# Gate and up biases copied into PSUM by ScalarE ahead of the first product, instead of one-hot products on TensorE

## The reference

```python
def clamped_swiglu(gu):
    gate, up = gu[..., :D_FF], gu[..., D_FF:]
    gate = jnp.minimum(gate, SWIGLU_LIMIT)
    up = jnp.clip(up, -SWIGLU_LIMIT, SWIGLU_LIMIT)
    return (up + 1.0) * (gate * jax.nn.sigmoid(SWIGLU_ALPHA * gate))
...
    def run_block(args):
        xb, e = args
        gu = xb @ w_gate_up[e] + b_gate_up[e]
        return clamped_swiglu(gu) @ w_down[e] + b_down[e]
```

## Time and profile before

| | us |
|---|---|
| timed runs (3) | 1540.11, 1543.22, 1545.4; median 1543.22 |
| the profiled execution: span from its first to its last instruction | 1541.1 |
| PE busy | 1519.2 (99%) |
| DVE busy | 1323.1 (86%) |
| ACT busy | 1092.0 (71%) |
| POOL busy | 238.7 (15%) |

### The profile page before, as it was taken

How to read it: one execution, slowest core, us unless ns; L and a number is a source line. 1 busy time by engine, 2 the same in 40 slices (tenths; PEclk the granted TensorE clock), 3 DMA queues, 4 the chain that set the end, 5 groups by cost and what they waited for, 6 DMA issues and landing times.

```text
span 1541.1 us, 21502 instructions
## 1 busy us (share of the span) xinstructions
PE 1519.2 (99%) x7332; PEld 1240.0 (80%) x7332; DVE 1323.1 (86%) x1056; ACT 1092.0 (71%) x1194; POOL 238.7 (15%) x170
## 2 busy tenths in 40 slices
PE   8999999998999999999999999999999999999997
PEld 6888789886888888888888888888888888888884
DVE  5586587747999999999999999999999999999985
ACT  6355587225777777777777777777777878777763
POOL 2611345300000011000000000011000001000111
PEclk9999999998999999999999999999999999999999
DMA  8330002446999999999999999999999999999973
GB/s 302 123 110 28 1 1 82 181 153 238 381 375 379 375 372 385 371 369 381 381 376 380 374 378 377 376 382 372 367 374 378 380 379 377 384 375 376 381 248 122
DMA packets 131102, 467.93 MB, mean 304 GB/s; under 512 B 12024, under 2 KB 12544, under 8 KB 130976
## 3 DMA queue, kind: packets, MB, share of 16 engines
q1 hardware_dynamic: 118720, 435.45, 74.1%
q0 software_dynamic: 9936, 27.01, 7.3%
q10 hardware_dynamic: 2416, 5.07, 0.9%
HBM read 452.81 MB, written 24.12 MB: 309 GB/s over the span
## 4 chain that ended last, share of the span: by engine, by line
PE 95%; DVE 2%; ACT 2%; issue 0%; DMA 0%; DVEq 0%; ACTq 0%
PE ps L1540 28%; PE ps L1542 28%; PE ps L1541 28%; PE ps L1853 2%; PE ps L1834 2%; PE ps L1826 2%; PE ps L1598 1%; PE ps L1641 1%; PE ps L1642 1%; PE ps L1771 0%; PE ps L1583 0%; DVE chunk_lo L1374 0%; ACT probs L815 0%; PE ps L1615 0%; PE ps L1616 0%; PE ps L1619 0%
## 5 line engine op out<-in xcount | busy, mean ns | idle before, releaser
L1374 DVE TENSOR_TENSOR chunk_lo<-chunk,chunk_hi 128x2048 fp32r<-128x2048 f32 x384 | 858.8, 2283 | 37.5 <-ACT chunk_hi L931 35.9
L931 ACT ACTIVATE chunk_hi<-chunk 128x2048 fp32r<-128x2048 f32 x378 | 723.1, 1914 | 103.6 <-PE ps L1542 103.6
L1540 PE MATMUL ps<-chunk_hi,XT 128*128 128x512 f32 x1024 | 404.1, 395 | 1.9 <-DVE XT L1416 1.9
L1542 PE MATMUL ps<-chunk_hi,XT 128*128 128x512 f32 x1024 | 399.5, 390 | 0.0
L1541 PE MATMUL ps<-chunk_lo,XT 128*128 128x512 f32 x1024 | 399.4, 390 | 0.0
L677 POOL DMA_INDIRECT sum_rows<-y,idx x31 | 81.4, 2626 | 952.8 <-ACT y L1059 863.7
L1540 PEld LDWEIGHTS ps<-chunk_hi,XT 128*128 128x128 f32 x1024 | 192.4, 188 | 40.9 <-DVE XT L1416 2.4
L1542 PEld LDWEIGHTS ps<-chunk_hi,XT 128*128 128x128 f32 x1024 | 192.2, 188 | 40.3
L1541 PEld LDWEIGHTS ps<-chunk_lo,XT 128*128 128x128 f32 x1024 | 192.5, 188 | 38.7
L1540 PE MATMUL ps<-chunk_hi,hidT 128*128 128x512 f32 x512 | 199.3, 389 | 0.5 <-DVE hidT L1423 0.5
L1541 PE MATMUL ps<-chunk_lo,hidT 128*128 128x512 f32 x512 | 199.2, 389 | 0.0
(11 more groups left out here) (288 smaller groups left out, 1949.8 us busy)
## 6 DMA issues: line engine op xcount, KB each, us to landing
chunk<-in_w_gate_up SPq DMA_DIRECT2D x256, 1024.0 KB, 8.4
chunk<-in_w_down SPq DMA_DIRECT2D x128, 1024.0 KB, 6.8
raw<-in_w_in SPq DMA_DIRECT2D x14, 1024.0 KB, 5.1
xs<-in_x SPq DMA_DIRECT2D x8, 512.0 KB, 6.4
w_out<-in_w_out SPq DMA_DIRECT2D x4, 1024.0 KB, 6.1
raw<-in_w_branch_a SPq DMA_DIRECT2D x2, 1024.0 KB, 5.4
raw<-in_w_branch_b SPq DMA_DIRECT2D x2, 1024.0 KB, 6.2
sum_rows<-xs ACTq DMA_DIRECT2D x4, 512.0 KB, 2.6
```

The costliest lines, as they stand in the source:

```text
L931: a.activation(chunk_hi[hi_slot(c, nxt)][:, :], chunk[c][:, :], ACT.Copy).then_inc(ex_hi, 1)
L1374: v.tensor_tensor(chunk_lo[c][:, :], chunk[c][:, :], chunk_hi[hi_slot(c, nxt, first)][:, :].bitcast(F32), ALU.subtract).then_inc(ex_lo, 1)
L1540: mm(dst, lhsT(0), rhs(0), start=start, stop=False)
L1542: return mm(dst, lhsT(1), rhs(0), start=False, stop=stop)
```

## The change

The bias products, `pick`, the bias table, its preparation on POOL, its store and its load go. In their place:

- SP loads the expert's gate bias and up bias, one row of 1024 float32 each, into one partition of `bias_rows` (the first expert's into `bias_first`): the gate row ahead of the loads of chunks 0 to 3, the up row ahead of those of chunks 4 to 7.
- POOL spreads each row over 128 partitions of `bias_all` (`partition_broadcast`), after the gather of the item has landed and ahead of the scatter: first the up row of the next expert, then the gate row of the one after that.
- ACT copies the spread rows into PSUM: `seed_gate` into banks 0 and 1 behind `rows_out`, `seed_up` into banks 2 and 3, with 1 added, behind the split of `hidT`.
- PE waits for these copies instead of adding the bias, and its first product of a bank adds to what lies there. For the banks to be in the adding state the first time, three filler products are made in them (`bits_set`).
- The scatter counter starts one DMA lower (`ADDED`), and a few start semaphores are joined.

```diff
@@ -181,7 +179,7 @@
...
-        ADDED = 3 * 16
+        ADDED = 2 * 16
...
@@ -345,6 +343,16 @@
...
+        def load_gate_row(sp, n, e):
+            sp.wait_ge(spread_g, n)
+            sp.dma_start(bias_rows[32:33, :], b_gate_up[0, bass.ds(e, 1), 0:FF]).then_inc(row_g_in, 16)
+        def load_up_row(sp, n, e):
+            sp.wait_ge(spread_u, n)
+            sp.dma_start(bias_rows[64:65, :], b_gate_up[0, bass.ds(e, 1), FF:2 * FF]).then_inc(row_u_in, 16)
         def load_expert(sp, c, e):
             sp.dma_start(chunk[c][:, :].rearrange("p (k n) -> p k n", k=2), expert_src(e, c)).then_inc(expert_in[c], 16)
@@ -449,6 +457,8 @@
...
             sp.wait_ge(merged, KD)
+            sp.dma_start(bias_first[32:33, :], b_gate_up[0, 0:1, 0:FF]).then_inc(row_g_in, 16)
+            sp.dma_start(bias_first[64:65, :], b_gate_up[0, 0:1, FF:2 * FF]).then_inc(row_u_in, 16)
             load_expert(sp, 1, 0)
...
@@ -457,11 +467,11 @@
...
             sp.wait_ge(gathered, 16)
             for c in range(8, 12):
                 load_expert(sp, c, 0)
+            load_gate_row(sp, 1, 1)
+            load_up_row(sp, 1, 1)
             for c in range(4):
                 sp.wait_ge(ex_used, c + 3)
                 load_expert(sp, c, 1)
...
@@ -472,12 +482,14 @@
...
                 load_expert(sp, c, 1)
             with sp.Fori(1, last_item) as i:
+                load_gate_row(sp, i + 1, (i + 1) % E)
                 for c in range(4):
                     sp.wait_ge(ex_used, 12 * i + c - 1)
                     load_expert(sp, c, (i + 1) % E)
                 for c in range(8, 12):
                     sp.wait_ge(ex_used, 12 * i + c - 5)
                     load_expert(sp, c, i % E)
+                load_up_row(sp, i + 1, (i + 1) % E)
                 for c in range(4, 8):
                     sp.wait_ge(ex_used, 12 * i + c + 3)
...
@@ -533,42 +544,9 @@
...
             pool.dma_start(acc[SEQ:ROWS, :], zeros[:, :]).then_inc(scattered, 16)
-
-
-            for q in range(3):
-                rows = slice(32 * q, 32 * q + 32)
-                pool.dma_start(bias32[rows, :], b_gate_up[0]).then_inc(bias_in, 16)
...
-            link(g.tensor_scalar(bias32[0:96, FF:2 * FF], bias32[0:96, FF:2 * FF], 1.0, None, ALU.add))
-            link(g.tensor_copy(bias_new[0:96, :], bias32[0:96, :]))
-            for rows in (part1, part2):
-                link(g.tensor_tensor(bias32[rows, :], bias32[rows, :], bias_new[rows, :], ALU.subtract))
-                link(g.tensor_copy(bias_new[rows, :], bias32[rows, :]))
-            link(g.tensor_tensor(bias32[part2, :], bias32[part2, :], bias_new[part2, :], ALU.subtract))
-            pool.dma_start(bias_parts, bias_new[:, :]).then_inc(scattered, 16)
@@ -645,6 +623,13 @@
...
+            pool.wait_ge(wout_ps, 2 * NT)
+            pool.wait_ge(row_g_in, 16)
+            g.partition_broadcast(bias_all[:, 0, :], bias_first[32:33, :]).then_inc(spread_g, 1)
+            pool.wait_ge(row_u_in, 16)
+            g.partition_broadcast(bias_all[:, 1, :], bias_first[64:65, :]).then_inc(spread_u, 1)
+            pool.wait_ge(spread_g, 1)
+            pool.wait_ge(spread_u, 1)
             pool.wait_ge(rows_stored, 2 * NT * 16)
             pool.wait_ge(scattered, ADDED)
...
@@ -652,12 +637,29 @@
...
+            def spread_gate(n):
+                pool.wait_ge(row_g_in, 16 * n + 16)
+                pool.wait_ge(gate_seeded, n)
+                pool.sem_inc(pool_past, 1)
+                g.partition_broadcast(bias_all[:, 0, :], bias_rows[32:33, :]).then_inc(spread_g, 1)
+            def spread_up(n):
+                pool.wait_ge(row_u_in, 16 * n + 16)
+                pool.wait_ge(up_seeded, n)
+                pool.sem_inc(pool_past, 1)
+                g.partition_broadcast(bias_all[:, 1, :], bias_rows[64:65, :]).then_inc(spread_u, 1)
             pool.wait_ge(idx_ready, 1)
             gather(0)
             pool.wait_ge(idx_ready, 2)
             pool.wait_ge(xt_ps, 1)
             pool.sem_inc(pool_past, 1)
             gather(1)
+            pool.wait_ge(gathered, 32)
+            spread_gate(1)
+            pool.wait_ge(spread_g, 2)
             pool.wait_ge(items_ready, 1)
             items = pool.value_load(items_i[0:1, 0:1], min_val=E, max_val=E * PASSES)
             lead = pool.value_load(items_i[0:1, 2:3], min_val=E - 4, max_val=E * PASSES - 4)
@@ -668,6 +670,15 @@
                 pool.wait_ge(xt_ps, n + 2)
                 pool.sem_inc(pool_past, 1)
                 gather((u + 2) % 4)
+            def spread_next(n, gate=True):
+                pool.wait_ge(gathered, 16 * n + 48)
+                spread_up(n + 1)
+                if gate:
+                    spread_gate(n + 2)
+                    pool.wait_ge(spread_g, n + 3)
+                pool.wait_ge(spread_u, n + 2)
             def scatter(n, u):
@@ -680,9 +691,11 @@
             with pool.Fori(0, lead, 4) as i4:
                 for u in range(4):
                     gather_ahead(i4 + u, u)
+                    spread_next(i4 + u)
                     scatter(i4 + u, u)
             for u in range(3):
                 gather_ahead(lead + u, u)
+                spread_next(lead + u, u < 2)
...
@@ -1007,6 +1020,26 @@
...
+            def seed_gate(n):
+                act.wait_ge(spread_g, n + 1)
+                if isinstance(n, int) and n == 0:
+                    act.wait_ge(bits_set, 1)
+                else:
+                    act.wait_ge(glu_ready, n)
+                a.activation(ps[0:CAP, 0:2, :].rearrange("p t n -> p (t n)"), bias_all[:, 0, :],
+                             ACT.Copy).then_inc(gate_seeded, 1)
+            def seed_up(n):
+                act.wait_ge(spread_u, n + 1)
+                if isinstance(n, int) and n == 0:
+                    act.wait_ge(bits_set, 2)
+                else:
+                    act.wait_ge(clip_ready, n)
+                a.activation(ps[0:CAP, 2:4, :].rearrange("p t n -> p (t n)"), bias_all[:, 1, :], ACT.Identity,
+                             bias=one[:, 0:1]).then_inc(up_seeded, 1)
             act.wait_ge(first_rows, 1)
             a.activation(f5[:, 0:2], idx_ps[:, 0:2], ACT.Copy).then_inc(first_f, 1)
             act.wait_ge(first_f, 1)
@@ -1029,6 +1062,7 @@
             act.wait_ge(idx_ready, 2)
             act.wait_ge(logits_ps, NT)
             index(2, slice(2, 3))
+            seed_gate(0)
             rows_hi(1, 0)
             rows_hi(1, 1)
             act.wait_ge(gateT_ps, 1)
@@ -1036,6 +1070,7 @@
             act.wait_ge(rows_stored, 2 * NT * 16)
             first_split_hi(4)
             first_split_hi(5)
+            seed_up(0)
             for c in (6, 7):
                 ex_split_hi(0, c)
             def sigmoid(used):
@@ -1067,6 +1102,7 @@
                 if before:
                     rows_out(i - 1, 12 * i + 6)
                 if nxt:
+                    seed_gate(i + 1)
                     ex_split_hi(i + 1, 2)
                     rows_hi(i + 2, 0)
                     ex_split_hi(i + 1, 3)
@@ -1083,6 +1119,8 @@
                     index_parts(i + 3, bass.ds((i + 3) % 4, 1))
                 ex_split_hi(i, 10, nxt)
                 hidden_hi(i + 1)
+                if nxt:
+                    seed_up(i + 1)
                 ex_split_hi(i, 11, nxt)
                 if nxt:
                     act.wait_ge(scattered, 16 * i + ADDED)
@@ -1796,9 +1832,12 @@
...
             pe.wait_ge(iota_set, 1)
+            for bank in range(2):
+                last = mm(ps[:, bank, :], onesb[:, :], iota_all[:, 0:256].bitcast(BF16), start=True, stop=True)
+            last.then_inc(bits_set, 1)
             for c in range(NT):
                 if c == NT - 1:
-                    unread(2, 1)
+                    unread(2, 2)
...
@@ -1843,30 +1882,23 @@
                     for t in range(2):
                         last = mm_split(ps[0:CAP, bank + t, :], lambda p: src[:, p, 2 * q + k, :],
                                         lambda p: expert_w(c, h, p, k, t),
-                                        start=(start and k == 0), stop=(stop and k == 1))
+                                        start=(start and k == 0), stop=(stop and k == 1), seeded=(bank < 4))
                 return last
-            def add_bias(e, bank, part, start=False):
-                for t in range(2):
-                    col = part * FF + t * 512
-                    mm(ps[0:CAP, bank + t, :], pick[:, bass.ds(e, 1)].to_broadcast([128, CAP]),
-                       bias_tab[:, col:col + 512], start=start, stop=False)
-            unread(3, 1)
+            unread(3, 2)
...
@@ -1874,18 +1906,19 @@
...
-                    add_bias(0, 0, 0)
-                weigh(c, c, c, XT, 0, c == 0, c == 3).then_inc(ex_used, 1)
-            pe.wait_ge(gateT_out, 1)
+                if c == 0:
+                    pe.wait_ge(gate_seeded, 1)
+                if c == 2:
+                    pe.wait_ge(gateT_out, 1)
```

(12 more changed lines are left out.)

89 lines of the change are left out of this document (30 added, 59 removed).

## The result

| | before | after |
|---|---|---|
| timed runs, median us | 1542.93 (1540.11 to 1545.4, 4 runs) | 1576.24 (1574.14 to 1581.11, 4 runs) |
| profiled execution, span us | 1541.1 | 1576.3 |
| PE busy | 1519.2 (99%) | 1517.7 (96%) |
| POOL busy | 238.7 (15%) | 473.6 (30%) |

The change makes the kernel slower: ratio 1.0224, 95% interval 1.021 to 1.0239. I had forecast 1515.2 with a range of 1510 to 1545. The time is 61 us above the one and 31 above the end of the other. All ratios are made of fast runs; two slow ones of the kernel before (2475.32 and 8758.93 us, beside e10 to e13) are left out.

The account below looks back on a forecast made before the run. PE was taken to set the pace at 35.47 us an expert. Span 1541.1 - 28.8 for bias products + 0.8 for fillers = 1513.1; from the timed 1543.2, less 28.0, 1515.2 us, range 1510 to 1545.

Parts of the forecast that it names:

- the one on the up seed: ACT's copy of the up bias could delay chunk 11's split by 1.05 us plus its row wait; cost on path 0.
- Bias products: On PE, 64 pairs of bias products at 0.45 us go, all on the chain: 28.8 us saved.
- the fillers' 0.8: Three filler products on PE at the start, 0.25 us each, rounded up to +0.8 us if all on the path.
- Seeds 1.05 us each: 64 ACT copies from SBUF to PSUM, 2.1 us an expert within 7.69 idle; cost on path 0.
- Spread 1.2 us: One GpSimd spread of a bias row over partitions takes 1.2 us, with 2.6 kept as the upper figure.
- DVE held for 1.2 us an expert: One spread holds up one DVE split; DVE then needs 34.4 of 34.57 us an expert, cost 0.
- Loads: SP's weight loads plus two 4 KB rows would keep up at 386 GB/s, with some 9 us in hand.
- Transfers that bind: Rival: 376 GB/s is all there is, so the beat falls back to 35.47 us; 1534 us, chance 0.10.
- both spreads on DVE: Rival: both spreads of an expert hold up DVE splits, DVE needs 35.6 us; 1544 us, chance 0.13.
- the long spread: Rival: a spread takes 2.6 us, holding DVE; 1551 us with one hit, about 1625 with two; chance 0.10.
- the third: Third rival listed: a spread of 2.6 us holds up DVE's splits, 1551 to about 1625 us; chance 0.10.
- PE waiting for a seed: Sign named as showing the forecast wrong: PE waits for ACT's copy of a bias into PSUM; no size given.

Follow-up runs that it names:

- e10: Changed kernel, with DVE waiting for its own previous split before the second and third of its three splits in a row: 1520.65 us, ratio 0.9853.
- e13: Changed kernel with both the up seed moved behind the split of chunk 5 and DVE waiting for its own splits: 1520.86 us, ratio 0.9852.
- e5: Changed kernel with the up seed later in ACT's queue, behind the split of the next expert's chunk 5: 1515.8 us, ratio 0.9818.
- e12: Kernel before the change, with two unused 128x512 reductions on DVE at the start of each item, so its splits begin later: 1541.25 us, ratio 0.9991.
- e11: Changed kernel with a 128x1 copy on DVE between the splits of chunks 0, 1 and 2: 1518.5 us, ratio 0.984.
- e2: Changed kernel with all row loads and spreads made, but seeds reading the first expert's gate row and never waiting for a spread: 1517.56 us, ratio 0.9838.
- e1: Changed kernel without spreads and row loads in the loop, every expert seeded with the first expert's rows: 1515.17 us, ratio 0.9816.
- e8: Changed kernel with the up seed one place later on ACT, behind the split of chunk 11 instead of ahead: 1525.67 us, ratio 0.9889.

## Why the prediction was wrong

**The step that failed** is the one on the up seed: "What it can delay is the split of chunk 11, queued behind it, by 1.05 us and whatever it waits for its row. ... Cost on the path: 0". I gave the seed's own 1.05 us a price and none to its wait, though the spread it waits for stands on POOL behind the scatter, which waits for ACT's `y`, and the next `y` stands twelve places behind the seed in ACT's own queue. Each wait had been placed in time (731.5 for the landing), always with the beat of before, and the circle was never added up. The rows shown would have given all of it but the last piece, which I take from the trace after: `y` at 716.07, gather at 721.55, landed 9.9 later, a spread of 1.2 to 2.3, the seed 1.05, and from there ACT's queue to the next `y`, 14.1 us all but without a pause (1375.4 to 1389.53): together 31.7 to 32.8 us, an estimate, against a beat of 34.57. It was closed, with 1.8 to 2.9 us in hand. That e5, which only takes the wait out of the way of the splits, brings 60 us shows that this step was it.

**What ate these 2 to 3 us** is the scatter: 6.76 us in place of 2.63, which alone makes 35.9 to 37.0, where 36.85 is the measured mean. In the expert of 37.46 the landing adds 0.8, with 10.72 in place of 9.9. I had weighed how long POOL can hold DVE up, and not how long DVE's splits can hold POOL up. e12 makes the scatter long in the kernel before, e10 and e11 make it short in the changed one and give back 56 and 58 us, and e2 has it short with all spreads in place (most of its scatters come ahead of the splits). It takes both: the circle (e12: long scatters alone cost nothing) and the starved scatter (e10, e11: the circle alone costs nothing to speak of). The Trainium skill (SBUF — State Buffer, "Who interferes with whom") says that a DMA which seems stalled by DVE is one whose descriptors GpSimd writes, which the runs bear out: the one held up here, 6.76 us in place of 2.63, is issued on GpSimd. It also has it that `tensor_tensor` was not seen to stall DMA, and infers that descriptors need the write side of the shared pair of ports. Here `tensor_tensor` with both inputs from SBUF holds the scatter off, for up to three splits; the measurement decides. The scatter also reads its row numbers (`idx`), and no run tells whether it is this or the descriptors that is held.

**Terms of the sum.**
- Bias products, 28.8 us: right, with the fillers' 0.8 not measured by itself. e1 is 27.8 under the kernel before, and its beat in the scatters' starts is 34.6 us (1020.46, 1055.05, 1089.64).
- Seeds 1.05 us each: 1.02 for the gate, 1.12 for the up half, hidden (e1).
- Spread 1.2 us: the operation takes 1.30; up to 3.45 where it waits for a split.
- DVE held for 1.2 us an expert: mis-sized. In e5 all splits together take 913.9 us, in e1 861.6 without spreads, so the spreads hold DVE for 52.3 / 31 = 1.7 us an expert, more than the 1.37 from which I had DVE decide. DVE stands at 34.67 of 34.70 us in e5, where an expert of e1 takes 34.59: the kernel gets off with about 0.1 us each. In the changed kernel itself the splits take 863.4 us and the price fell on POOL (a spread of 2.26 behind a split).

```profile
L1403 DVE TENSOR_TENSOR chunk_lo<-chunk,chunk_hi 128x2048 fp32r<-128x2048 f32 x384 | 861.6, 2285 | 30.1 <-issue 20.0
L1411 DVE TENSOR_TENSOR chunk_lo<-chunk,chunk_hi 128x2048 fp32r<-128x2048 f32 x384 | 913.9, 2425 | 5.6 <-ACT chunk_hi L944 3.7
```

- Loads: right. e5 moves 390 GB/s, where 386 were asked, and its chain has 0% of DMA.
- Sum 1515.2: what e1 and e5 measure (1515.17, 1515.8). The sum was that of a kernel whose circle is open. That it fits to half a microsecond is luck, since e5's four runs lie 8 us apart.

**The rivals.** None was this one. Transfers that bind and both spreads on DVE are excluded by e2 and e5, and the long spread by its 1.30 us. The form of the third was right (an engine held up at the shared place, slower than before), with the engines the wrong way round. Among the signs that would show me wrong I had named "PE waiting for a seed"; it was ACT that waited for a spread.

## What to carry to other kernels

When an edit adds a wait, follow it backwards through the queues until it leaves the item or comes back to its own engine. If it comes back, add up the circle and compare it with the beat; here 2 to 3 us in hand were no cover. An indirect DMA that GpSimd issues during a run of DVE instructions with two SBUF inputs should be priced up to the end of the run, not at the duration it had before; here a copy of 0.14 us between them let it through, and asked for just ahead of the run it was not held up in 83 cases of 90. Put an instruction that waits for a long chain as late in its queue as its reader allows, behind work that doesn't need it.

## What the runs showed of the hardware

- A scatter that is asked for during a split on DVE ends 1.44 to 1.53 us behind the end of one (334 of 341). Between two splits that follow each other with the second one's input there for 0.14 us or more, it was let in 2 times of 55 in the changed kernel and in none of 59 in e12; with a wait or a 128x1 copy between them, 38 times of 38 (e10, e11).
- That isn't a strict rule. In e2, e5 and e8 the next split had been ready for 0.9 us and more at all 45 such gaps, and 15 were taken (8 of 14 in e2, 2 of 10 in e5, 5 of 21 in e8). What decides there is open.
- Asked for up to 0.3 us ahead of the first split, the scatter took 1.60 to 1.85 us in 83 cases of 90 (e2, e5, e8, e10, e11, e13) and the split ran beside it. What decides in the other seven is open.
- What the circle would be without POOL's wait for the gather's landing (10.7 us, its longest piece) was not tried: the spread would then run beside a gather still under way.
